# Eight expert buffers, a loop body of two pairs, an fp32 token gather and late gate weights in a mixture-of-experts encoder layer

## What is computed

```python
x = x + concat(hgrn(h), conv(h)) @ w_out             # h = rmsnorm(x) @ w_in, 1024 -> 3072
h2 = rmsnorm(x, norm_ffn)
top_val, top_idx = top_k(h2 @ w_router + b_router, 4)  # 4 of 32 experts
gates = softmax(top_val)
for each chosen expert e of a token:
    gu = h2 @ w_gate_up[e] + b_gate_up[e]            # 1024 -> 2048
    gate, up = min(gu[:1024], 7), clip(gu[1024:], -7, 7)
    hid = (up + 1) * gate * sigmoid(1.702 * gate)
    x += gates[e] * (hid @ w_down[e] + b_down[e])    # 1024 -> 1024
x = x + sigmoid(rmsnorm(x) @ w_ple_gate) * (p @ w_ple)
y = rmsnorm(x)
```

## Time and profile before

| | us |
|---|---|
| median of three runs | 1218.29 |
| lowest, highest | 1217.98, 1221.67 |
| the profiled execution | 1219.33 |
| its span | 1217.5 |

### The profile page before, as it was taken

How to read it: one execution, slowest core, us unless ns; L and a number is a source line. 1 busy time by engine, 2 the same in 40 slices (tenths; PEclk the granted TensorE clock), 3 DMA queues, 4 the chain that set the end, 5 groups by cost and what they waited for, 6 DMA issues and landing times.

```text
span 1217.5 us, 14744 instructions
## 1 busy us (share of the span) xinstructions
PE 1125.7 (92%) x5871; PEld 462.0 (38%) x5871; DVE 387.3 (32%) x838; ACT 232.8 (19%) x370; POOL 39.5 (3%) x23
## 2 busy tenths in 40 slices
PE   5999989899999999999989898989898989899986
PEld 4775655433333333333323232323232323233333
DVE  5568975621313212121212121212130303031234
ACT  3531114412020101111111111111202020211124
POOL 3340000100000000000000000000000000000000
PEclk9998999699999999999999999999999999999998
DMA  9913121699999999999999999999999999999911
GB/s 288 365 37 139 43 104 42 239 386 430 428 427 428 430 428 428 428 430 427 429 428 429 428 428 428 430 428 429 428 429 428 429 428 430 428 428 428 427 44 39
DMA packets 44057, 430.73 MB, mean 354 GB/s; under 512 B 4885, under 2 KB 8933, under 8 KB 19359
## 3 DMA queue, kind: packets, MB, share of 16 engines
q1 hardware_dynamic: 39016, 425.42, 83.7%
q10 hardware_dynamic: 5015, 4.95, 1.2%
HBM read 428.53 MB, written 1.83 MB: 353 GB/s over the span
## 4 chain that ended last, share of the span: by engine, by line
PE 68%; DMA 26%; DVE 3%; ACT 1%; issue 1%; SPq 0%; ACTq 0%; DVEq 0%
PE ps L779 34%; DMA ring<-in_w_gate_up 24%; PE ps L480 7%; PE ps L470 5%; PE ps L739 5%; PE ps L704 4%; PE ps L798 4%; DMA ring<-in_w_down 2%; PE ps L714 2%; PE ps L788 1%; PE ps L504 1%; PE ps L747 1%; PE ps L544 1%; PE ps L562 1%; PE ps L706 1%
## 5 line engine op out<-in xcount | busy, mean ns | idle before, releaser
L779 PE MATMUL ps<-ring,arena 128*64 128x512 f32 x2048 | 466.7, 598 | 19.4 <-DMA ring<-in_w_gate_up 19.4
L798 PE MATMUL ps<-ring,arena 128*64 128x512 f32 x1024 | 232.3, 598 | 30.8 <-DMA ring<-in_w_down 13.6
L779 PEld LDWEIGHTS ps<-ring,arena 128*64 128x64 f32 x2048 | 136.5, 137 | 296.0 <-issue 255.7
L798 PEld LDWEIGHTS ps<-ring,arena 128*64 128x64 f32 x1024 | 68.5, 137 | 171.2 <-issue 113.6
L1694 DVE TENSOR_TENSOR acc<-ps,acc 128x512 f32<-128x512 f32 x64 | 44.2, 691 | 212.8 <-PE ps L739 212.8
L1580 DVE CAST arena<-cst 96x128 bf16 (+1 forms) x17 | 3.8, 222 | 273.0 <-PE ps L779 273.0
L1104 ACT COPY arena<-ps 128x512 f32<-128x512 f32 x32 | 18.7, 586 | 328.9 <-PE ps L788 328.9
L480 PE MATMUL ps<-ring,arena 128*128 128x512 f32 x140 | 64.3, 615 | 1.1 <-DVE arena L1472 1.1
L470 PE MATMUL ps<-arena,ring 128*128 128x288 f32 x256 | 64.2, 410 | 0.7 <-DVE arena L1249 0.7
L1599 DVE TENSOR_TENSOR arena<-ps,par 128x256 f32<-128x256 f32 x68 | 25.5, 417 | 121.5 <-PE ps L779 118.4
L739 PE MATMUL ps<-arena 128*128 128x512 f32 x128 | 63.5, 619 | 0.0
(11 more groups left out here) (267 smaller groups left out, 799.9 us busy)
## 6 DMA issues: line engine op xcount, KB each, us to landing
ring<-in_w_gate_up SPq DMA_DIRECT2D x128, 2048.0 KB, 24.4
ring<-in_w_down SPq DMA_DIRECT2D x64, 2048.0 KB, 23.1
ring<-in_w_in SPq DMA_DIRECT2D x5, 2048.0 KB, 20.5
ring<-in_w_out SPq DMA_DIRECT2D x2, 2048.0 KB, 15.8
ring<-in_w_in SPq DMA_DIRECT2D x2, 1024.0 KB, 11.9
arena<-in_w_ple_gate ACTq DMA_DIRECT2D x2, 768.0 KB, 5.6
arena<-in_w_ple_gate ACTq DMA_DIRECT2D x1, 1280.0 KB, 10.2
acc<-in_x_prompt SPq DMA_DIRECT2D x2, 512.0 KB, 4.5
```

Of the source, the lines that this page charges most:

```text
L779: t = mm(ps[h * 64:h * 64 + 64, G + 2 * e + g, :], xT[:, 2 * kk + c, e * 64:e * 64 + 64], w[:, c, lo:lo + 512], start=False, stop=(kk == 3 ...
L798: t = mm(ps[n * 64:n * 64 + 64, PP + e, :], hidT[:, 4 * e + c, half * 64:half * 64 + 64], w[:, c, n * 512:(n + 1) * 512], start=(half == 0 ...
```

## The change

- **Eight buffers for expert units** instead of six. Six of the places are the ring's; the two others (`beside`) are a part of the arena that the recurrence and the convolution used, and 4096 columns per partition by which the arena grows. Unit u uses place `u % 8` with a semaphore of its own. The first eight units have conditions of their own; afterwards unit u waits for `unit_done` of unit u - 8.
- **Loop body of two pairs** on SP and PE (24 units, three rounds of eight places) in place of one pair.
- **Gather in fp32.** `xn2` is now the stationary operand, read with a step of two elements, and the selection, in fp32, the moving one: 8 x 3 matmuls with 128 columns write the gathered tokens already turned. `turn_tokens`, `copy_gathered`, the bf16 parts and the casts and subtractions that made them are removed, and two copies of the sample's positions.
- **Gate weights at the end.** All of `w_ple_gate` comes in two transfers of 2048 KB on SP's queue behind the last expert unit, into places 0 and 1.
- **Smaller reserve** for dynamic DMA (1024 bytes), which makes room for the larger arena.

```diff
-RING = 6 ... LEAD = 9 ... EARLY = 5 ... FREE = 5
+RING = 6 ... SLOTS_E = 8 ... BODY = 24
-        ARENA = 15248
+        ARENA = 18416
+        beside = [arena[:, A_Q:A_Q + UNIT], ex(UNIT)]
+        landed_in = [sem(f"expert_in{i}") for i in range(SLOTS_E)]
+        def place_of(u):
+            at = u % SLOTS_E
+            return beside[1 - (at - 3)] if at in (3, 4) else slot((3, 4, 5, 0, 0, 0, 1, 2)[at])
+        gate0, gate1 = (place_of(n).rearrange("p (c n) -> p c n", c=DC) for n in range(2))
@@ SP
-            before = {0: ("proj_mm", PROJ_DONE[3]), 1: ("proj_mm", PROJ_DONE[4]), 2: ("proj_mm", PROJ_DONE[5]),
-                      3: ("out_mm", 6), 4: ("out_mm", 6), 5: ("pl_mm", 6)}
+            free = [("proj_mm", PROJ_DONE[3]), ("proj_mm", PROJ_DONE[4]), ("proj_mm", PROJ_DONE[5]),
+                    ("lev_done", NLEV), ("mixc_ready", H), ("out_mm", 6), ("out_mm", 6), ("pl_mm", 6)]
+            for u in range(BODY):
+                if u < SLOTS_E:
+                    sp.wait_ge(S[free[u][0]], free[u][1])
+                else:
+                    sp.wait_ge(S["unit_done"], u - SLOTS_E + 1)
+                expert_unit(u // PER * 2, u % PER, u)
+            with sp.Fori(1, PAIRS // 2) as jj:
+                for u in range(BODY):
+                    sp.wait_ge(S["unit_done"], jj * BODY + (u - SLOTS_E + 1))
+                    expert_unit(jj * 4 + u // PER * 2, u % PER, u)
-            sp.dma_start(slot(LEAD)[:, 0:(DC - EARLY) * W]...)
+            for n in range(2):
+                sp.wait_ge(S["unit_done"], steps * PER + (n + 1 - SLOTS_E))
+                sp.dma_start((gate0, gate1)[n], a["w_ple_gate"][0, :, n * W:(n + 1) * W].rearrange(
+                    "(c p) n -> p c n", p=P)).then_inc(S[f"gate_in{n}"], 16)
@@ PE, gather
-                for n in range(2):
-                    for b in range(2):
-                        for k in range(3):
-                            mm(ps[:, PP + n, :], selb[:, b, :], xsb[:, b, k, cols],
-                               start=(b == 0 and k == 0), stop=False)
-                    mm(ps[:, PP + n, :], selb[0:96, 2, :], xssb[0:96, cols],
-                       start=False, stop=True).then_inc(S["gath_mm"], 1)
-            def turn_tokens(j): ...
-            pe.wait_ge(S["xs_l"], NB)
+                for c in range(DC):
+                    lo = 256 * (c // 2) + c % 2
+                    for b in range(NB):
+                        t = mm(ps[:, PP + c // 4, (c % 4) * P:(c % 4 + 1) * P],
+                               xn2[0:ROWS[b], b, lo:lo + 255:2], sel[0:ROWS[b], b, :],
+                               start=(b == 0), stop=(b == NB - 1), skip_group_check=True)
+                    if c % 4 == 3:
+                        t.then_inc(S["gath_mm"], 1)
+            pe.wait_ge(S["xn2_ready"], NB)
@@ PE, loop
-            with pe.Fori(0, PAIRS) as j:
-                step(j)
+            with pe.Fori(0, PAIRS // 2) as jj:
+                for half in range(2):
+                    step(jj * 2 + half, lambda s: jj * (16 * BODY // SLOTS_E), half * PER)
@@ ACT
-            gate_chunks(...)                                   # four calls
-            high(b), middle(b), low(b), copy_gathered(j)
@@ POOL
-            G.tensor_tensor(rest, rest, xssb[0:DEC, :], ALU.subtract)
-            G.tensor_tensor(rest, rest, mtmp, ALU.subtract)
@@ DVE
-            remainder(0, 0), remainder(0, 1), remainder(1, 0), remainder(1, 1)
-            V.tensor_copy(posm[DEC:2 * DEC, 2, 0:E], posm[0:DEC, 2, 0:E])
-            link(V.tensor_copy(posm[2 * DEC:3 * DEC, 2, 0:E], posm[0:DEC, 2, 0:E]))
-                    dve.wait_ge(S["xt3_mm"], j * 2 + (n + 1))
+                    dve.wait_ge(S["gath_mm"], j * 2 + (n + 1))
@@ kernel
-    nc = bacc.Bacc("TRN2", target_bir_lowering=False, num_devices=1)
+    nc = bacc.Bacc("TRN2", target_bir_lowering=False, num_devices=1, dynamic_dma_scratch_size=1024)
```

More of the change, by code:

```diff
@@ L244, in ex @@
             return arena[:, at2[0] - n:at2[0]]
-        gath = ex(D)
         xT = blocks(ex(D), DC)
+        selg = blocks(ex(NB * P))
+        oneh = ex(P // 2).bitcast(BF16)
+        ex(64)
+        gw = ex(T)
+        ex(D - 64 - T - NB * P - P // 2)
         gbuf, sgm, ubuf = ex(D), ex(D), ex(D)
@@ L750, in combine_sample, with step @@
                 t.then_inc(S["comb_mm"], 1)
-            def step(j):
+            def step(j, body, at):
                 pe.wait_ge(S["oneh_ready"], j + 1)
@@ L767, in landed @@
                 def landed(k):
-                    u = LEAD + k
-                    pe.wait_ge(full[u % RING], j * (16 * PER // RING) + 16 * (u // RING + 1))
+                    u = at + k
+                    pe.wait_ge(landed_in[u % SLOTS_E], body(u % SLOTS_E) + 16 * (u // SLOTS_E + 1))
                 def gate_up(k):
@@ L840, in _ @@
                 with pe.Fori(0, n_more) as i:
-                    step(i + PAIRS)
+                    step(i + PAIRS, lambda s: i * (32, 16)[s < 4] + (16 * PAIRS * PER // SLOTS_E - (16, 32)[s < 4]), PER)
             steps = n_more + PAIRS
@@ L865, in _ @@
                         t.then_inc(S["x3t_mm"], 1)
-            pe.wait_ge(S["gate_in"], 16 * 4)
-            late = slot(LEAD)[:, 0:(DC - EARLY) * W].rearrange("p (c n) -> p c n", n=W)
             for b in range(NB):
                 pe.wait_ge(S["h3_ready"], 2 * b + 2)
-                row_block(h3T, gate0, b, PG_BANK[2 * b], range(DC), DC - 1).then_inc(S["pg_mm"], 1)
-                row_block(h3T, gate1, b, PG_BANK[2 * b + 1], range(EARLY), DC - 1)
-                if b == 0:
-                    pe.wait_ge(full[LEAD % RING], steps * (16 * PER // RING) + 16 * (LEAD // RING + 1))
-                row_block(h3T, late, b, PG_BANK[2 * b + 1], range(EARLY, DC), DC - 1, EARLY
-                          ).then_inc(S["pg_mm"], 1)
+                for n in range(2):
+                    if b == 0:
+                        pe.wait_ge(S[f"gate_in{n}"], 16)
+                    row_block(h3T, (gate0, gate1)[n], b, PG_BANK[2 * b + n], range(DC), DC - 1
+                              ).then_inc(S["pg_mm"], 1)
         @block.scalar
@@ L1057, in _ @@
             root(1, 0)
-            high(0)
-            middle(0)
             tokens_hi(0)
             square_of(1)
-            low(0)
             square_of(2)
@@ L1509, in _ @@
             normalise(0)
-            remainder(0, 0)
             residual(1)
             tokens_lo(0)
-            remainder(0, 1)
             residual(2)
@@ L1520, in _ @@
             normalise(2)
-            remainder(1, 0)
             zero_rest(lg[:, 2, :])
@@ L1543, in _ @@
             zero_rest(msk[:, 2, :]).then_inc(S["msk_ready"], 1)
-            remainder(1, 1)
             dve.wait_ge(S["pos_mm"], 1)
```

121 lines of the change are left out of this document (17 added, 104 removed).

## The result

The changed kernel is slower: 1245.89 us in the median of four runs (1240.32 to 1250.2), beside 1219.98 us for the kernel before; the ratio is 1.020, with an interval of 1.014 to 1.027, so it is slower beyond the noise, and whether by more or less than 2% is open. The profiled execution took 1249.88 us, with a span of 1248.1, that is 30.6 us more than before. The forecast was 1209.4 us, with a range of 1203 to 1245: it had the wrong sign, and the median lies 0.9 us above the range.

What follows compares the result with a forecast made beforehand. The expert loop was taken as DMA-bound, with 3.7 us of PE slack per step. Buffers -9.8, later third buffer +2.9 and earlier start -2.0 gave -8.9 us: 1210.4 profiled, 1209.4 median, range 1203 to 1245.

Steps and rivals of the forecast that it cites:

- The bound now: Expert loop: DMA-bound at 58.74 us a step against PE's 55.0, leaving PE 3.7 us of slack.
- rival A: Expert loop: PE becomes the bound; time 1230 at 0.16 us per record, 1266 at 0.209; chance 0.23.
- The new gather on PE: Each expert step: 4.29 us removed, 5.96 added for 48 records, so PE's step becomes 56.7 us, under 58.74.
- 0.20 us once: Fp32 gather: fixed term of 0.20 us, derived from two groups of turns, added once to 48 x 0.12.
- -2.0 in front: Ahead of the expert loop: the start comes 2.0 us earlier, bounds -4.6 and +1.1.
- The range: Whole time: 1203 to 1245 us, the top taking in rival A up to about 0.17 per record.
- Two more buffers: Expert loop: 184 units left instead of 186 at 4.895 us each, so -9.8 us.
- The hole at the third unit: First expert step: third buffer comes free later, DMA hole 3.2 us instead of 0.3; net +2.9, bounds 0 and 6.
- The way into the first step: DVE chain before the loop 3.3 us shorter, gather from 225.3 to 233.9 with its clock rising midway; start -2.0 us.
- Gate weights at the end: Behind the last expert unit: two transfers land before PE needs them; cost 0, at least 2.8 us margin.
- Body and reserve: Loop body of two pairs: 0, bound up to 1 us per turn (8 us); smaller reserve: no cost.

Runs made afterwards that it cites:

- the second look at the kernel: The changed kernel run again unchanged, for a second profile and the clock during the first gather; measured 1242.24 us, span 1240.4.

## Why the prediction was wrong, step by step

**The bound now.** Right. PE had 3.7 us of slack per step, and the whole forecast hung on them. The threshold of rival A, 57.3 us, lies between what was measured: at 56.45 the late loop is on DMA, at 57.98 every step is on PE and the gain is gone.

**The new gather on PE: the step that failed.** The record's price was right, and it was the number that I took to be the unknown: 48 records without a change take 5.85 us, forecast 5.96. The failed term is the "0.20 us once" in 48 x 0.12 + 0.20. I took it from two groups of turns, which have one height throughout, read it as the price of beginning a group, and counted it once. Its size was right and its count was wrong: it is paid at the beginning of every run of tiles of one height. The gather goes 128, 128, 32, 128, 128, 32 rows and has 16 such runs; 48 x 0.118 + 16 x 0.19 = 8.7 us, and 8.75 is measured. The same sum with 9, 2 and 1 runs gives the 7.40, 6.04 and 5.85 us of the other three kernels to 0.03 us. I had L544 with 32 rows at 0.113 a record and concluded that low tiles need no term of their own. The row shows only low tiles among themselves, and the run with the low blocks last confirms just that.

With the measured step the prediction's own formula for rival A gives 16 x 59.34 = 949.4 us for the loop, +25.2 against 924.2, and with the -2.0 in front 1218.29 + 23.2 = 1241.5: the second look at the kernel took 1242.24. So the sum was sound and one of its terms too small by 2.8 us (8.75 against 5.96), on a path where 2.0 us were left (58.74 - 56.7). Rival A was named at 0.23, but I tied it to the price of a record and to loads of 209 ns. Both were beside the point: the loads last 195 to 200 ns in the changed kernel and 196 with 128-row blocks, and overlap among tiles of one height in both.

The reading of the earlier trace rows was also too broad. The 209, 208 and 140 ns are all loads of turns. The load of a matmul lasts 189 ns without any step (L739 of the kernel before, first row), and in the new gather 196 with a step of two (128-row blocks, second row), so there the step lengthens a load by 7 ns and not by 69:

```profile
L739 PEld LDWEIGHTS ps<-arena 128*128 128x128 f32 x128 | 21.7, 189 | 41.3 <-issue 41.3
L707 PEld LDWEIGHTS ps<-sam,xs 128*128 128x128 f32 x816 | 97.4, 196 | 14.4 <-issue 14.4
```

The Trainium skill (TensorE: Matmul & The Clock Gate, Part 3, "The mechanism") has weight loads overlap running matmuls when they target another row group or the background weight buffer, and adds that they overlap only when the row group differs. The runs here fit the first by its background buffer and not the second: loads of one height overlap (0.12 us from load to load, each 0.196 long). Neither says what the loads show at a change from 128 to 32 rows or back, a start 0.20 us later than that.

**The range.** Its top was 1245, and the median came 0.9 us above it. I described the top as rival A up to 0.17 us a record; by the prediction's own sum 0.17 gives 1237, and 1245 belongs to 0.18 (8.75/48 is 0.182). The measured step alone gives the 1241.5 above, inside the range. Two of the four times lie inside it (1240.32 and 1241.89). The profiled execution lies above it: against the second look its gathers ahead of the first step and in it cost 4.4 us more and the stretch from the last unit to the end 3.2 (60.2 us and 57.0), both at the lower clock. So the bound was put on the wrong quantity, and it left no room for the clock on top.

**Two more buffers.** Right: -9.8 forecast; 9.1 and 9.9 in the loop of the kernel with the old gather, 8.8 between eight and six places (9.4 by the ratios). In the changed kernel itself they bring nothing, since PE leads from the first step.

**The hole at the third unit.** With 128-row blocks the time from the first to the last unit of the loop is 912.4 us (233.04 to 1145.44), 8.2 less than before, and with the old gather 9.1 less. So what the new gather costs here is about 0.9 us and not 2.9; the lower bound, 0, was nearer. The third unit is issued 16.4 us after the loop's start (249.39), as forecast (16.5). I didn't isolate why this costs less than the hole would.

**The way into the first step.** The chain on DVE came out as worked: the gather starts at 224.93 (225.3 forecast), and the one-hot takes 0.56 us without POOL beside it, not 2.49.

```profile
220.36 0.56 DVE L1464 TENSOR_TENSOR arena<-cst,small 128x384 f32<-128x384 f32 x1
```

Behind it the clock decides. With the gather at 2.4 GHz and no changes of height the loop starts at 233.04, 5.1 us earlier (my bound was -4.6), and in the changed kernel at 241.27 or 237.82, 3.2 later or 0.3 earlier. The assumption that the clock rises 5.3 us after the gather begins has no counterpart: it fell during the gather in one execution and held in the other.

**Gate weights at the end: the second failed step.** I wrote 0, because the data queues are idle there and the weights land in time. Both are true, and I had looked only at who needs the weights, not at who else needs the queues. It costs a stop of 4 us plus matmuls at 1.2 GHz. From the last unit to the end the kernel before needs 58.8 us and the four with the gate weights in the way 64.8, 64.0, 63.1 and 62.9; with the wait it is 57.1, 57.2 and 60.4. Of the 5.8 us between 62.9 and 57.1, the stop has 2.8 (4.10 against 1.27) and the eight slow matmuls 3.0. Without the stop this stretch takes 57.0 to 60.5 us in the kernels and executions profiled; the two of the changed kernel, 57.0 and 60.2, differ by the clock alone. In whole times it is 4.3 us where nothing else was changed (ratio 1.0039), and with and without the wait 5.3 and 7.7 us between medians, 4.3 and 7.1 by the ratios, in which the clock ahead of the loop may have a part. The changed kernel hides this error. There PE is so late that the gate weights have long landed (issued at 1161.19, the loop ends at 1191.45), and its first work behind the loop waits 1.27 us only.

**Body and reserve.** Right: 1.0008 and 1.0009.

**Two errors that cancel.** With 128-row blocks the span is 9.2 us shorter than before, and the forecast was -8.9. It looks like a confirmation and is none: the loop was 1.3 us better than forecast, the front 3.1 us better, and the tail 4.0 worse (62.9 us from the last unit against 58.8).

**Open.** Why the clock falls during the first gather in one execution and not in another wasn't found. That the gate weights in the queues make the stop is shown: it is there in the four kernels that have them there and in none of the other nine. That it is a load of code is supported by its place and by the instruction packet, which comes 2.6 to 2.8 us later, as much as the stop is longer, with PE following 1.8 us behind its end. But no view names the engine that the packet is for or what PE waited for, and PE also reads a word of a table there (`n_more`), which was not tested by itself. How much the fp32 gather brings by itself lies between 0.7 and 4.0 us.

## What to carry to other kernels

Before counting records by a price, write down the heights of consecutive weight tiles: a group that alternates 128-row and 32-row tiles pays about 0.19 us at each change, and padding the short block to its neighbours' height, or taking all short blocks last, removes it without saving a single record. When DMA leads by a few per cent, work out the step at which the other engine takes over and compare it with every addition's upper bound, over the whole group and not only per record. And don't start a bulk transfer where an engine leaves a loop, even if the data queue is idle there: here it delayed an instruction packet and cost 4 us of a stop.

## What was not expected of the hardware

Eight 32-row tiles (16 records) among 128-row tiles make a gather of 48 fp32 records 50% longer (8.75 against 5.85 us), although it moves less data and each record alone is no slower.

A stop of 4.0 to 4.2 us on PE at the exit of a loop while the queues carry 386 to 390 GB/s of data, in four kernels with bodies of one pair and of two; 1.3 to 1.6 us, which ACT's copies take, in the nine others. The eight matmuls behind the stop took 5.3 to 6.7 us in all four and 3.7 us in all nine others, and the granted clock was 0.50 in the window behind it with 128-row blocks.

Without the stop the clock can still fall a few microseconds later, or not. The first window is from the kernel that holds the gate weights back, the second from the one that does so with the old gather, 12 us after PE begins its last unit in both:

```profile
1155.00:1160.00 5.00, 4.41 (x18) 3.31 (x19) 4.67 (x18) 3.04 (x6) 0.00 (x0) 0.56 1.05 387
1159.00:1164.00 5.00, 4.51 (x23) 2.83 (x24) 4.36 (x18) 3.01 (x6) 0.00 (x0) 1.00 1.05 388
```

PE was about as busy in both and the queues carried the same data. The first execution needs 60.4 us from its last unit to the end and the second 57.2.
